# Reordering the sixteen expert turns of a fused decoder layer

## The reference

```python
gate = jnp.sum(jax.nn.one_hot(top_idx, N_EXPERTS, dtype=jnp.float32) * top_w[..., None], axis=-2).astype(h.dtype)
y = jnp.zeros_like(h)
for e in range(N_EXPERTS):
    he = jax.nn.silu(h @ w_e_gate[e]) * (h @ w_e_up[e])
    y = y + gate[..., e:e + 1] * (he @ w_e_down[e])
```

## Time and profile before

| | us |
|---|---|
| Runs | 1248.67, 1253.16, 1253.0 |
| Median | 1253.0 |
| The profiled execution, its own time | 1253.86 |
| Its span in the trace | 1251.7 |
| TensorE busy | 1072.2 (86%) |
| VectorE busy | 471.6 (38%) |
| Stretch of the expert turns, first to last matmul | 896.60 to 1203.38 |
| End of the program behind it | 1203.38 to 1251.7 |

### The profile page before, as it was taken

How to read it: one execution, slowest core, us unless ns; L and a number is a source line. 1 busy time by engine, 2 the same in 40 slices (tenths; PEclk the granted TensorE clock), 3 DMA queues, 4 the chain that set the end, 5 groups by cost and what they waited for, 6 DMA issues and landing times. The chain is left out here.

```text
span 1251.7 us, 21771 instructions
## 1 busy us (share of the span) xinstructions
PE 1072.2 (86%) x8838; PEld 720.9 (58%) x8838; DVE 471.6 (38%) x1175; ACT 179.0 (14%) x437; POOL 255.2 (20%) x306
## 2 busy tenths in 40 slices
PE   2699999976899998999997999993799999997940
PEld 1477777434576766777875775443555555554520
DVE  0111699912237887654111201445313211110108
ACT  1200012102122221211110110000011111111101
POOL 2200014475121222232122441000000000000034
PEclk9779999997999999999897999995599999998975
DMA  9964435347503215120027106415188999999944
GB/s 296 308 93 57 135 136 198 109 146 252 195 21 114 60 45 179 34 71 23 5 80 168 68 1 214 164 42 210 51 305 298 364 354 364 385 393 396 366 138 131
DMA packets 120538, 218.12 MB, mean 174 GB/s; under 512 B 23600, under 2 KB 42407, under 8 KB 120437
## 3 DMA queue, kind: packets, MB, share of 16 engines
q1 hardware_dynamic: 97380, 180.95, 41.9%
q10 hardware_dynamic: 17129, 16.66, 5.7%
q0 software_dynamic: 5936, 19.16, 4.8%
HBM read 196.07 MB, written 21.04 MB: 173 GB/s over the span
## 5 line engine op out<-in xcount | busy, mean ns | idle before, releaser
L1546 PE MATMUL bank<-arena 128*128 128x288 f32 (+8 forms) x2512 | 652.6, 420 | 47.6 <-DVEq L1213 14.3
L1546 PEld LDWEIGHTS bank<-arena 128*128 128x128 f32 (+2 forms) x2512 | 451.3, 194 | 235.3 <-issue 140.6
L1854 PE MATMUL bank<-arena 128*32 128x256 f32 x3136 | 185.9, 389 | 15.1 <-issue 11.8
L1854 PEld LDWEIGHTS bank<-arena 128*32 128x32 f32 x3136 | 104.4, 111 | 88.5 <-issue 23.1
L1501 DVE TENSOR_TENSOR arena<-arena,bank 128x128 f32<-128x128 f32 x49 | 14.2, 290 | 252.5 <-ACT arena L1025 252.5
L1875 PE MATMUL bank<-arena 128*32 128x256 f32 x1568 | 94.6, 381 | 0.0
L766 POOL TENSOR_SCALAR arena<-arena 128x288 f32<-128x288 f32 x48 | 45.3, 944 | 237.2 <-ACT arena L991 237.2
L1550 PE MATMUL bank<-arena 128*128 128x128 f32 (+5 forms) x327 | 51.1, 289 | 40.8 <-DVE arena L1320 19.9
L1096 DVE SCALAR_TENSOR_TENSOR arena<-arena 128x512 f32<-128x512 f32 x120 | 81.9, 743 | 0.0
L1550 PEld LDWEIGHTS bank<-arena 128*128 128x128 f32 (+5 forms) x327 | 37.9, 154 | 59.1 <-issue 24.2
L817 POOL DMA_INDIRECT arena<-h,ints x13 | 13.5, 1038 | 272.2 <-PE bank L1836 229.5
(11 more groups left out here) (240 smaller groups left out, 736.7 us busy)
## 6 DMA issues: line engine op xcount, KB each, us to landing
arena<-in_w_e_gate SPq DMA_DIRECT2D x16, 2048.0 KB, 12.1
arena<-in_w_e_up SPq DMA_DIRECT2D x16, 2048.0 KB, 15.7
arena<-in_w_e_down SPq DMA_DIRECT2D x16, 2048.0 KB, 11.1
arena<-in_w_ada SPq DMA_DIRECT2D x12, 2048.0 KB, 12.7
arena<-in_w_in SPq DMA_DIRECT2D x10, 2048.0 KB, 9.5
expert_rows<-arena POOLq DMA_DIRECT2D x1, 5120.0 KB, 17.3
arena<-in_x_prompt SPq DMA_DIRECT2D x8, 512.0 KB, 8.7
arena<-in_w_o SPq DMA_DIRECT2D x2, 2048.0 KB, 8.2
```

The source lines that it names most:

```text
L1546: last = pe.matmul(out, a, b, start=k == 0, stop=k == len(pairs_) - 1)
L1854: last = pe.matmul(out, HG[:, g % 2, k, a:a + BLK], gate_up[i % 2][:, :, k, c * P:c * P + P], start=k == 0, stop=k == KT - 1)
```

## The change

The table `TURNS` gets another order, and the rows of the last turn are zeroed along with the others, with one more DMA on POOL and one more increment in the waits. By the blocks of each turn, before: 3, 3, 5, 2, 5, 2, 4, 2, 4, 3, 3, 3, 2, 3, 3, 2. After: 3, 3, 2, 5, 2, 4, 2, 4, 2, 3, 2, 3, 3, 3, 3, 5.

```diff
-TURNS = [0, 1, 2, 11, 3, 12, 4, 13, 5, 6, 7, 8, 14, 9, 10, 15]
+TURNS = [0, 1, 11, 3, 12, 4, 13, 5, 14, 6, 15, 7, 8, 9, 10, 2]
...
+                    pool.dma_start(y_d[FIRST[NE - 1] * BLK:NBLK * BLK].rearrange("(p b) (h d) -> p (b h) d", p=BLK, d=512),
+                                   ZERO[0:BLK].unsqueeze(1).broadcast_to([BLK, 2 * NB_AT[NE - 1], 512])).then_inc(ev("far_zeroed"), 16)
...
                 if (x, f, h) == ("A", KT - 1, 0):
-                    pool.wait_ge(ev("far_zeroed"), 32)
+                    pool.wait_ge(ev("far_zeroed"), 48)
...
                 if d == 0:
                     act.wait_ge(ev("weights_up"), 1)
+                    act.wait_ge(ev("far_zeroed"), 48)
...
-            act.wait_ge(ev("far_zeroed"), 32)
+            act.wait_ge(ev("far_zeroed"), 48)
```

## The result

| | before | changed |
|---|---|---|
| Median, us | 1253.08 (4 runs) | 1261.87 (4 runs, 1259.76 to 1263.85) |
| Ratio, 95% interval | | 1.0078 [1.0051, 1.0106] |
| The profiled execution, its own time | 1253.86 | 1259.76 |
| Its span in the trace | 1251.7 | 1257.6 |
| First to last matmul of the expert turns | 896.60 to 1203.38, 306.78 | 893.01 to 1214.96, 321.95 |

The changed kernel is 8.8 us slower by the medians. Its turns take 15.2 us longer, its tail is 5.7 us shorter. The turns began 3.6 us earlier in this execution; over all fourteen profiles here the start lies between 890.49 and 896.60, so that is scatter, and I compare lengths, not ends.

A forecast was written before the change was run, and what follows sets the result against it. TensorE and the DMA engines were taken to share the limit, weight loads on average the slower side. Turns +14.8, tail -3.3, zeroing +0.7 made 12.2 us more: 1266.1 for the profiled execution, 1265 as median, range 1256 to 1275.

The forecast's parts named there:

- The turns: Expert turns in the new order: seven waits for weights, 23.3 us, plus 8.5 of slow clock; 14.8 us more than before.
- the rules: Three rules per turn: when TensorE is ready, when SP's queue is released, when weights land; waits of 2.3 us add 1.7.
- the bounds of 12.4 and 16.5: Lower and upper ends, in us, for the extra time of the expert turns, forecast at 14.8.
- near 1219: Sign in the changed kernel's timeline: when the last matmul ends, from 1203.4 + 14.8 + 0.7.
- The tail: After the last matmul: earlier first gathers and adding gathers waiting for the last write alone, 3.3 us less.
- the 7.4 us: In the tail: time from the last write's issue to the adding gathers, taken from the old kernel's write-to-first-gather time.
- The bounds of 1 and 6: Lower and upper limits, in us, for the gain after the last matmul, forecast at 3.3.
- The zeroing: One more POOL issue in a stretch where TensorE waits for VectorE: 0.7 us more, bounds 0 and 1.3.
- A: Rival for the turns: landings come earlier and TensorE never waits, decided at turn 3; 1231 us, chance 0.08.
- B: Rival for the turns: waits at turns 3, 5, 7 but none at 9 and 11; a draw, 1249 us, chance 0.12.
- C: Rival: later landings, longer slow clock after turns 5 and 11, tail gains 1 us; 1270 to 1274 us, chance 0.20.
- the prediction's bound of 2.3: At a turn's start: a TensorE wait of 2.3 us or more was taken to add 1.7 us of slow clock.

The follow-up runs named there:

- tables last: Changed kernel with the four layer-norm tables loaded behind the last weights and the two VectorE steps using them moved behind the block loop: 1261.29 us, ratio 1.0063.
- gathers held: Changed kernel with the first gathers held until the last turn's rows are written: 1275.51 us, ratio 1.0177; with half-loaded weights as well, 1242.01 us, 0.9908.
- gathers paced: Changed kernel with each first gather issued only when the one before has landed: 1266.53 us, ratio 1.0108.
- tables at turn 4: Changed kernel with the four layer-norm tables loaded ahead of turn 4's weights instead of turn 5's: 1262.99 us, ratio 1.0075.
- the two other orders: The change's code with other turn orders: first with the tables kept ahead of turn 5, 1251.64 us (0.9981); second with them loaded last, 1247.73 us (0.9960).

## Why the prediction was right

The forecast was 1265, 12.2 us slower; the measurement is 1261.87, 8.8 us slower, and 13.3 us slower in the second set of runs of the same kernel (1266.37 against 1253.09). Slower by more than 0.5% was given 0.79.

**The turns: +14.8 predicted, +15.2 in the trace.** The cause named is shown: half the bytes take away all waits but one of 0.5 us in both orders; the place of the tables alone costs the old order 4 to 5 us; removing them from under the short turn shortens the turns by about 3 in the traces; and an order picked by the same rules, with the tables last, beats the old one. The waits one by one:

| Turn | 3 | 5 | 7 | 9 | 10 | 11 | 12 | 13 | 14 | 15 |
|---|---|---|---|---|---|---|---|---|---|---|
| predicted | 3.4 | 7.2 | 2.5 | 2.5 | 0 | 6.3 | 0 | 0 | 0.4 | 1.0 |
| measured | 5.05 | 8.80 | 2.11 | 2.50 | 3.98 | 2.46 | 1.69 | 0.66 | 0.34 | 0 |

Turns 3 and 5 were 1.6 us worse each, 7 and 9 within 0.4. At turn 10 the rules had a tie, landing 1091.1 against ready 1091.3; it waited 3.98, and turn 11 for the rest, together 6.4 where 6.3 stood at turn 11 alone. The backlog was sized right and its place was not. It then ran on to turns 12 and 13. All in all 27.6 against 23.3, and the clock 7.0 against 8.5: three slow groups of 2.3 us each, not five of 1.7 (after 2.1 to 2.5 us it did not fall at turns 7, 9 and 11, while in the second trace of the same kernel it did at turn 11, behind 3.48). The rules were 2.8 us short in all here, and 2.4 short before; the two errors largely cancel in the difference, which is why I compared rule with rule. 15.2 lies inside the bounds of 12.4 and 16.5, but how close it is to 14.8 is luck: without the first blocks' 1.4 us it would be at the upper bound. That the last matmul ended at 1214.96 and not near 1219 is for the most part the earlier start.

**The tail: -3.3 predicted, -5.7 in the trace.** This term was mis-sized. The step that failed is the 7.4 us that I took for the landing of the last write, plus 0.7 for its size. The adding gathers started 5.4 us after its issue, 6.0 us behind the last matmul and not 9.1. What the 7.4 us held besides the landing stands in the trace of before, POOL's branches between the write (issued from 1200.10) and the first gather (1207.50):

```profile
L834 POOLq COMPARE_BRANCH  x10: 45/45/45, 1205.2 to 1206.6; - x10
```

These branches ask, behind the wait for the writes, whether there are further tiles. So the writes had landed some 5 us after their issue, and 2.4 us were POOL's way to the first gather. The adding gathers have no such branches ahead of them, and in the new order POOL has passed them inside the last turn. It was not traffic on the DMA engines: with the gathers held, the last write has as little beside it as in the changed kernel, and the first gather comes 8.0 us after its issue, with the same ten branches from 1226.4 to 1227.8. The first adding gather then took 6.2 us where I had 5.5. The bounds of 1 and 6 hold it.

**What the tail gave, the last turn took back in some executions.** I had costed the first gathers inside the last turn at nothing. In the second trace of the changed kernel they cost 2.9 us. 324.91 - 306.78 = 18.1 us of turns and -5.0 of tail make +13.1 there, and the ratio of that set is 1.0108. In the first set, without this, the trace makes 15.2 - 5.7 = +9.5, and the ratio is 1.0078. That the same cost explains the medians is not shown, since only one execution of each set was profiled.

**The zeroing: +0.7 predicted.** From the start of L722 to the matmul behind the wait it is 14.80 us before and 15.37 after, 0.57 more, and 15.38 with the zeroing alone; the new issue on POOL took 0.75. In the total of that run it cannot be seen.

**The rivals.** A (no waits, 1231) fell at turn 3, which waited 5.05. B (a draw, 1249) was to be decided at turn 11; turns 9, 10 and 11 all waited. C (1270 to 1274) had much of its turns right: landings a little later than by the rules, and slow groups of 2.3 us where before they cost 1.7, though three and not five. But the tail gained 5.7 us where C gave it 1.

By the fit for one DMA in the Trainium skill (DMA: Bandwidth & Descriptors, Anatomy of one DMA), the old order would have had no waits and the new one 12.0 us of them, says the prediction; by its own three rules the 12.0 are, as an estimate, about 9 us of waits and 3.4 of slow clock. The traces show 14.25 and 27.6 us of waits. The page gives the fit for DMAs that POOL issues, and here it understates the loads of SP's queue, as the trace of before had said.

## What to carry to other kernels

When loads are released by the consumer's progress, cost an order turn by turn, as the later of "queue free" and "released", and ask what else rides in the queue under the shortest turn; evenness of the mean says nothing. Compare the rule's result for both orders, not one with a measurement. And count work that a change starts earlier, here the gathers, as a load on what it now runs beside. When a time between two events is carried over to another place, look at what else lies in it: 2.4 of the 7.4 us here were branches of the waiting engine.

## What the hardware showed that I had not expected

**TensorE held up in the middle of a block, beside a burst of gathers.** In the last turn nothing is loaded any more and all inputs are there, and yet the time from the last transposed tile to the last matmul took two values: 18.07 us in before, in the first trace of the changed kernel, with gathers held and with gathers paced; 21.54, 21.42, 21.01 and 21.11 in four kernels whose five first gathers ran there back to back (tables at turn 4, tables last, the changed kernel again, half the weights). The second trace of the changed kernel, TensorE:

```profile
1201.59 4.21 PE L1858 MATMUL bank<-arena 128*32 128x256 f32 x64
1205.99 0.63 PE L1879 MATMUL bank<-arena 128*32 128x256 f32 x5
1207.34 0.63 PE L1879 MATMUL bank<-arena 128*32 128x256 f32 x4 [0.72 <-issue]
1208.76 1.31 PE L1879 MATMUL bank<-arena 128*32 128x256 f32 x20 [0.79 <-issue]
```

The same stretch of it in the windows view (PE busy is the second number):

```profile
1205.00:1210.00 5.00, 3.49 (x39) 1.71 (x39) 0.49 (x2) 0.28 (x1) 2.02 (x3) 1.00 0.90 310
```

A `down` group of 32 matmuls, 1.93 us elsewhere, is torn into pieces, with idle time for which the trace shows no semaphore; the clock stayed at 1.00. The gathers were issued from 1201.74 to 1206.72 there. Where the gathers are held or paced, it did not happen in any of the three kernels profiled; where they run back to back, in four of five. In the first of the two other orders they began only 3.4 us ahead of the last matmul; TensorE lost 0.2 us, and ScalarE the 3.8 us shown above. So by these nine traces the burst looks needed for it, and is not enough, and it is not TensorE alone that it meets.

The cause is open. One suspicion was that TensorE ran out of fetched instructions while the gathers filled the DMA engines: in the kernel with the tables at turn 4 the DMA view of 1198 to 1206, in which the blocks are torn, has no packet of the queue marked instruction, and its next one lies in 1206 to 1208. But two things in the traces speak against it. From 1206.20 on TensorE ran 61 matmuls at full pace, and that packet starts only at 1207.6. And in the old order with half the weights nine microseconds, 1110 to 1119, pass without such a packet, while TensorE is busy without a break (the windows view above). The whole of that DMA view's queues:

```profile
q1 hardware_dynamic: 914, 2.33, 80.7%
q10 hardware_dynamic: 448, 0.39, 13.1%
q0 software_dynamic: 17, 0.07, 1.9%
```

The weights' own loads, which keep the engines as full (share 1.04 in the earlier trace rows), never tore a block. One more thing sets the five held-up traces apart: a gather's landing is recorded as 16 steps of a semaphore, and in these traces, and in no other, only 6 to 14 of them are recorded for each of the first three gathers. Whether the lost records and the hold-up have one cause, and whether the taking of the profile has a part in it, no run here tests.

**A wait near 2.4 us can go either way with the clock.** Over the kernels with whole weights, none of the 13 waits from 1.6 to 2.34 us was followed by a slow first group, and each of those from 2.63 us up was. Between them both happened: after 2.37 (twice), 2.43 (twice) and 2.47 us the 64 matmuls took about 5.3, after 2.40, 2.45, 2.46, 2.50 and 2.52 they took 3.66. So the same wait costs nothing or 1.7 us beside itself, and the prediction's bound of 2.3 sat just under that band. Longer waits cost 1.3 to 2.9 us, not always 1.7.
